# One hybrid decoder layer on eight cores: weights loaded as plain f32 and cast on ScalarE, VectorE and GpSimd, and attention's division moved into the retention stage

## The reference

```python
xn = rmsnorm(x)
qa, ka, va, qr, kr, vr, gr, ga, gb = split(xn @ w_in)
# A: 16 heads of width 64, keys by stride, three patterns (window, dilation)
for w, r in ((128, 1), (512, 4), (2048, 16)):
    num += exp(s - m) @ v        # the three share one numerator
    den += sum(exp(s - m))       # and one denominator
y_att = (num / den) @ w_att
# B: 4 heads, keys 256 wide, values 512 wide, chunks of 128 positions
y = inner_decayed @ v + (q * xi) @ state;  state = state * gamma + (k * zeta).T @ v
y_ret = (rmsnorm(y) * silu(gr)) @ w_ret
x = x + (sigmoid(ga) * y_att + sigmoid(gb) * y_ret) @ w_out
x = x + moe(rmsnorm(x))          # 4 groups of 8 experts, top 2 of the top group
```

## Time and profile before

| | |
|---|---|
| median of the runs shown | 1613.28 us (1604.24 to 1700.53, 3 runs) |
| the profiled execution itself | 1600.68 us |
| its span, first to last instruction, slowest core | 1596.2 us |
| PE busy | 1371.4 us, 86% of the span |
| DVE, ACT, POOL busy | 765.3, 695.0, 763.7 us |
| DMA queue q0 (POOL) | 124.30 MB, 48.6% of the 16 DMA engines' time |
| DMA queue q1 (SP) | 140.76 MB, 28.2% |

### The profile page before, as it was taken

The page is one execution under the profiler, slowest core; times in us unless marked ns, Lnnn a source line. Parts: engine busy times, 40 slices in busy tenths (PEclk is TensorE's granted clock), DMA queues, the critical chain, the costliest instruction groups (busy, mean ns, idle before and its releaser), DMA issues.

```text
span 1596.2 us, 29866 instructions; the slowest of 8 cores (1581.8 to 1596.2 us)
## 1 busy us (share of the span) xinstructions
PE 1371.4 (86%) x10037; PEld 787.3 (49%) x10037; DVE 765.3 (48%) x1239; ACT 695.0 (44%) x1191; POOL 763.7 (48%) x874
## 2 busy tenths in 40 slices
PE   4889998888879999999999899999999746476575
PEld 2344447777654444444444344444445435355463
DVE  3687774767556656555656411111355662121122
ACT  3576667887753444434443411111233543223232
POOL 1379991332236657666756312221226645354353
PEclk9999998999999999999999899999999867788797
DMA  9747865777865678999984299785964785999985
GB/s 213 212 92 131 166 145 152 175 175 171 176 146 100 112 107 127 127 131 146 125 134 123 55 293 175 119 131 111 261 211 166 212 303 151 265 254 256 261 188 92
DMA packets 105502, 267.03 MB, mean 167 GB/s; under 512 B 43354, under 2 KB 65370, under 8 KB 98818
## 3 DMA queue, kind: packets, MB, share of 16 engines
q0 software_dynamic: 29280, 124.30, 48.6%
q1 hardware_dynamic: 76066, 140.76, 28.2%
HBM read 285.71 MB, written 116.65 MB: 252 GB/s over the span
## 4 chain that ended last, share of the span: by engine, by line
PE 69%; DMA 14%; DVE 4%; issue 4%; ACT 4%; POOL 3%; SPq 1%; POOLq 0%; DVEq 0%; ACTq 0%
PE ps L169 69%; DMA arena<-xn,idx 8%; DMA zret<-arena 5%; ACT arena L169 4%; DVE arena L169 3%; POOL arena L169 3%; DMA arena<-x 1%; DMA cfs_sb<-cfs 1%; SPq L169 1%; DVE arena L167 1%; DMA vp<-arena 0%; ACT L169 0%; DVEq L156 0%; DVE logit L169 0%; POOL wb L169 0%
## 5 line engine op out<-in xcount | busy, mean ns | idle before, releaser
L169 PE MATMUL ps<-arena 128*128 128x512 bf16 (+5 forms) x8208 | 1275.5, 313 | 75.1 <-ACT arena L169 30.2
L169 PEld LDWEIGHTS ps<-arena 128*128 128x128 bf16 (+1 forms) x8208 | 677.4, 102 | 583.4 <-issue 121.5
L169 ACT ACTIVATE arena<-ps 128x512 bf16<-128x512 f32 (+5 forms) x600 | 422.5, 719 | 445.8 <-PE ps L169 416.7
L169 POOL TENSOR_TENSOR arena<-arena 128x512 bf16<-128x512 f32 (+4 forms) x274 | 347.8, 1278 | 296.5 <-DVE arena L169 243.0
L169 DVE TENSOR_TENSOR arena<-ps,arena 128x512 f32<-128x512 f32 (+4 forms) x420 | 235.2, 572 | 337.9 <-PE ps L169 153.5
L169 PE MATMUL ps<-cbs_sb,arena 128*128 128x128 bf16 x1408 | 130.8, 232 | 111.6 <-DMA arena<-xn,idx 76.3
L169 DVE SCALAR_TENSOR_TENSOR arena<-arena,ps 128x512 f32<-128x512 f32 x176 | 115.6, 683 | 192.8 <-PE ps L169 191.3
L169 PEld LDWEIGHTS ps<-cbs_sb,arena 128*128 128x128 bf16 x1408 | 100.3, 104 | 180.8 <-issue 152.0
L169 ACT ACTIVATE arena<-arena 128x8 f32<-128x8 f32 (+5 forms) x225 | 148.6, 665 | 60.1 <-DVE arena L169 24.5
L169 DVE TENSOR_TENSOR arena<-arena 128x1024 bf16<-128x1024 bf16 (+9 forms) x176 | 131.7, 756 | 70.6 <-ACT arena L169 63.6
L169 POOL DMA_INDIRECT out<-arena,idx x48 | 76.3, 1591 | 122.8 <-ACT arena L169 68.8
(11 more groups left out here) (60 smaller groups left out, 340.6 us busy)
## 6 DMA issues: line engine op xcount, KB each, us to landing
wb<-wexp POOLq DMA_DIRECT2D x60, 768.0 KB, 16.0
arena<-wb SPq DMA_DIRECT2D x30, 1536.0 KB, 16.0
arena<-x SPq DMA_DIRECT2D x32, 512.0 KB, 7.2
arena<-vx POOLq DMA_DIRECT2D x12, 768.0 KB, 15.1
arena<-wri POOLq DMA_DIRECT2D x8, 1024.0 KB, 23.2
zret<-arena SPq DMA_DIRECT2D x16, 512.0 KB, 19.0
arena<-zret SPq DMA_DIRECT2D x4, 2048.0 KB, 17.2
out<-arena SPq DMA_DIRECT2D x16, 512.0 KB, 8.2
```

Source lines behind the costliest of these rows:

```text
L169: ins = getattr(engobj, meth)(*a, **kw)
```

## The change

Weights: a list of tasks of 128 x 1024 f32 (512 KB) each. `stage_load` issues the next task's plain DMA on SP into one of two (attention) or three (later) 4 KB buffers; `stage_cast` issues the cast into bf16, on POOL in attention, on ACT in retention, on DVE in the merge. Each of the two is called at fixed points: twice per head in attention, twice per step in retention, five times per unit in the merge. A cast comes two (attention) or three calls behind its load. Head 0 has 12 tasks, as has each other head; a merge block has 5, the output projection 8.

Division: after a head SP stores the numerators (f32, 512 KB) and one row of denominators to DRAM. In retention DVE inverts all denominators at once (step 1, 128 x 256), and 32 units of 128 x 512 follow: loads of numerators and broadcast denominators at step 4 + u (`div_load`, three DMAs), the multiply and the store four steps later (`div_mul`). `NDB` = 4 is the number of buffers.

Masks: of the four items of dilation 4 only places 3 and 5 keep the bias matmuls; 2 and 4 take DVE's mask.

Converts: 12 in the projections, none in attention, 31 in retention (every second step to 60), 17 in the merge.

```diff
+        def stage_load():
+            n = done[0]
+            if n < len(tasks) and n - done[1] < len(stg):
+                done[0] += 1
+                i = n % len(stg)
+                p.dma(stg[i], tasks[n][1], writes=[Rstg[i]], semkey=("stg", i))
+
+        def stage_cast(eng, lag):
+            n = done[1]
+            if n < done[0] and (done[0] - n >= lag or done[0] == len(tasks)):
+                done[1] += 1
+                dst, _, r_ = tasks[n]
...
+                if eng == "act":
+                    OP("act", "activation", out=dst, in_=stg[i], func=AF.Copy, reads=[Rstg[i]], writes=[r_])
+                else:
+                    OP(eng, "tensor_copy", out=dst, in_=stg[i], reads=[Rstg[i]], writes=[r_])
...
-            if 24 <= ucount[0] < 96 and ucount[0] % 9 == 0:
+            if 24 <= ucount[0] < 96 and ucount[0] % 6 == 0:
                 convert(1)
...
-        def den_act(pr, hf, func, scale):
-            OP("act", "activation", out=den[hf], in_=den[hf], func=func, scale=scale, reads=Rden[hf], writes=Rden[hf])
...
+        def head_out(pr, e):
+            h, r0, d0, i = 2 * pr + e, e * 64, 64 - e * 64, (2 * pr + e) % NXO
+            p.dma(num_d[h * 64:(h + 1) * 64, :], xo[i][r0:r0 + 64, :], reads=Rxo[i], writes=[Rnum[h]], semkey=("zatt", i))
+            p.dma(den_d[h:h + 1, :], xo[i][d0:d0 + 1, :], reads=Rxo[i], writes=[Rdend[h]], semkey=("xin", i))
...
-            load_cast(w.rearrange("p k n -> p (k n)"), wri_d[h, :, c0:c1], 1 + j // 2, Rwr[i][j], ("wr", i, j))
+            stage_add(w.rearrange("p k n -> p (k n)"), wri_d[h, :, c0:c1], Rwr[i][j])
...
-                    if n_ == 9:
-                        convert(1)
...
-            queue.append((pr, eh, n_, S_item(pr, eh, kind, j, n_ in (2, 3, 4, 5))))
+            queue.append((pr, eh, n_, S_item(pr, eh, kind, j, n_ in (3, 5))))
...
+            if n_ in (1, 6):
+                stage_cast("pool", 2)
+                stage_load()
...
+        def div_load(u):
+            pr, qt, i = u // 4, u % 4, u % NDB
...
+        def div_mul(u):
+            pr, qt, i = u // 4, u % 4, u % NDB
+            OP("dve", "tensor_tensor", out=zo[i], in0=nb[i], in1=rb[i], op=ALU.mult, reads=[Rnb[i]] + Rrb[i], writes=[Rzo[i]])
...
                 stage_A(s_)
+                stage_cast("act", 3)
+                stage_load()
...
+                stage_cast("act", 3)
+                stage_load()
+                if s_ == 1:
+                    den_rec()
+                ud = s_ - DIV0
+                if 0 <= ud - NDB < NDV:
+                    div_mul(ud - NDB)
+                if 0 <= ud < NDV:
+                    div_load(ud)
                 pending = pending[take:]
-                if s_ % 4 != 1 and s_ < 48:
+                if s_ % 2 == 0 and s_ <= 60:
                     convert(1)
...
                 piece(fc, c, n, 4 * (un % 2), 0, "pool")
+                stage_cast("dve", 3)
+                stage_load()
...
-            if 3 <= un <= 21 and un % 2:
+            if un <= 21 and (un % 4 or un == 0):
                 convert(1)
```

More of the change, by code:

```diff
@@ L336, in psb @@
             return ps[:, b, :].bitcast(BF16)
+        late_res = set()
         def OP(eng, meth, *a, reads=(), writes=(), **kw):
@@ L341, in MM @@
         def MM(out, lhsT, rhs, start, stop, reads, writes, **kw):
+            assert not late_res or all(id(r_) not in late_res for r_ in reads)
             return p.op("pe", "matmul", (out,), dict(lhsT=lhsT, rhs=rhs, start=start, stop=stop, **kw), reads, writes)
@@ L929, in pv_next @@
             if n_ == NB - 1:
-                todo.setdefault(g + 1, []).append(lambda: (osb_copy(pr, eh, 3), den_shift(pr, eh, 1)))
-                if eh == 1:
-                    for hf in range(2):
-                        for lag, f in ((1, lambda hf=hf: den_act(pr, hf, AF.Ln, 1.0)), (3, lambda hf=hf: den_act(pr, hf, AF.Exp, -1.0)),
-                                       (5, lambda hf=hf: z_out(pr, hf) if pr < 7 else deferred.append(lambda: z_out(pr, hf)))):
-                            todo.setdefault(g + lag + 4 * hf, []).append(f)
+                todo.setdefault(g + 1, []).append(lambda: (osb_copy(pr, eh, 3), head_out(pr, eh)))
         for pr in range(2):
@@ L991, in build_nc @@
         wr_alloc(1)
+        areset(92 * KB, 96 * KB)
+        stb = [alloc([128, 1024], F32, [Rstg[0]])]
+        areset(192 * KB)
+        stb += [alloc([128, 1024], F32, [Rstg[i]]) for i in (1, 2)]
+        stage_init(stb)
         areset(112 * KB)
@@ L1138, in build_nc @@
         NWM = 3
-        Rwm = [[p.res(f"wm{i}_{j}") for j in range(2)] for i in range(NWM)]
+        Rwm = [[p.res(f"wm{i}_{j}") for j in range(5)] for i in range(NWM)]
         wm = []
@@ L1205, in build_nc @@
         wm.append(alloc([128, 40, 128], BF16, Rwm[2]))
+        stage_init([alloc([128, 1024], F32, [Rstg[i]]) for i in range(3)])
         load_wm(2)
@@ L1209, in build_nc @@
         mT = [alloc([128, 8, 512], BF16, RmT[c]) for c in range(NG)]
-        Rwo = [p.res(f"wo{i}") for i in range(2)]
-        wo = [alloc([128, 8, 512], BF16, [Rwo[0]])]
+        Rwo = [[p.res(f"wo{i}_{j}") for j in range(4)] for i in range(2)]
+        wo = [alloc([128, 8, 512], BF16, Rwo[0])]
         areset(192 * KB)
-        wo.append(alloc([128, 8, 512], BF16, [Rwo[1]]))
+        wo.append(alloc([128, 8, 512], BF16, Rwo[1]))
         Rsga = [p.res(f"sga{i}") for i in range(2)]
@@ L1223, in build_nc @@
         WMH = (slice(0, 16), slice(16, 40))
+        WMC = (slice(0, 2), slice(2, 5))
         def keep_wm(fc):
```

108 lines of the change are left out of this document (65 added, 43 removed).

## The result

The changed kernel takes 1678.19 us (median of 4 runs, 1671.34 to 1692.6) against 1611.15 us: the ratio is 1.044 with a 95% interval of [1.035, 1.054], so it is **slower**. The span of the slowest core goes from 1596.2 to 1678.8 us.

What follows compares the result with a forecast made beforehand. PE bounds retention and merge; in attention PE and ACT are both near their limit. Terms -21 - 1 - 8 + 1 + 2 + 4 + 8 + 1 = -14 us, off 1604, give 1590 us, range 1562 to 1622.

Steps and rivals of the forecast that it cites:

- The division leaves attention, -21: Attention: without the division PE's waits of 15.0 us for ACT and 5.8 us for DVE go, -21 us.
- seven divisions at 3.6 us: Attention: an alternative estimate of the division's gain, 25 us, set aside for the waits seen.
- Two of four bias pairs go, -8: Attention: dropping bias matmuls saves 12.2 us of PE, of which -8 us (0 to -12) was taken.
- Projections, +1: Projections: four more converts cost POOL 2.4 us beside its normalisation work, +1 us (0 to +3).
- Retention: DMA, +4 (0 to +25): Retention, where heads load: 17.7 us of transfers in two steps of 13.5 us, a loss of +4 us.
- ACT can lag unnoticed: Retention: ACT, idle half of the time, can lag some microseconds behind late pieces without harm.
- Merge, +8 and +1: Merge: PE waits at the first cast, +8 us (0 to +20); later blocks' pieces, +1 us (0 to +10).
- A unit and a half of slack: Merge: later blocks' pieces compete with 17 converts for 10 but have this slack, so only +1 us.
- Multiplies on DVE, +2: Retention: 32 added DVE multiplies can stand ahead of something PE needs, +2 us, bounds 0 and 28.
- The rival that they lock out POOL: Retention: DVE's multiplies delay POOL, +28 in place of +2, 1616 us in all; chance 0.08.
- The rival of the late pieces: Retention: f32 pieces come late, ACT waits and holds PE; slower than before, +20, 1624 us; chance 0.1.
- the 9.1 at which ACT waits: Retention: with three pieces in flight, landing time in us from which the late piece decides the pace.

Runs made afterwards that it cites:

- bias4: The changed kernel with all four dilation-4 items of a head keeping their bias matmuls and DVE's 32 masks for them gone; ratio to the kernel before 1.045.
- best4: best3 with conversions spread evenly (9, 6, 35, 10 by stage) and the division's store a step after its multiply; 1585.43 us against 1605.16, ratio 0.986.
- best4b: best4 with conversions 12, 6, 31, 11 by stage, four fewer in retention and three more in the projections; ratio to the kernel before 0.987.
- no_div: The changed kernel without the loads and multiplies of 28 of the 32 division units in retention; ratio to the kernel before 1.018.
- best3_f32: best3 with the division's numerators and inverses in f32 again, 32 units of 128 x 512 at the same gaps; ratio to the kernel before 1.035.
- r_cast_gap: The changed kernel with r_cast's edit and the f32 division units at steps away from the heads' loads; ratio to the kernel before 1.019.
- best3: Kernel before plus bf16 division in retention away from heads' loads, two bias pairs gone, only head 0 staged, conversions as before (8, 6, 36, 10); ratio 1.012.
- r_cast: The changed kernel with heads 1 to 3 and merge blocks 0 and 1 again loaded with a conversion in the transfer; ratio to the kernel before 1.034.
- after_sp: The changed kernel with division units loaded into buffers multiplied a step earlier, and stored a step after their multiply; ratio to the kernel before 1.043.
- cv_att: The changed kernel with six conversions moved from the merge back into attention, 11 in the merge for 17; ratio to the kernel before 1.033.
- best2_ms: The changed kernel with bf16 division away from heads' loads, conversions 12 in attention, 30 in retention, ten in the merge, merge still staged; ratio to kernel before 1.018.
- best3_ls: best3 with only the division unit's store issued a step after its multiply, conversions unchanged; ratio to the kernel before 1.005.
- gap_bf16: Changed kernel, bf16 division away from heads' loads, conversions 8, 6, 36, 10, later merge and output weights converted in transfer; 1616.9 and 1617.1 us against 1605.1, unclear.

## Why the prediction was wrong

- **The division leaves attention, -21**: right, and a little small: some 27 by bias4. The 25 of "seven divisions at 3.6 us", which I had set aside, was nearer.
- **Two of four bias pairs go, -8**: mis-sized, 1 to 4. That attention as a whole came within 2 us of its forecast is luck: this term was too large by about what the one before was too small. PE was busy 11 us less (191.8 of 216.5 us, against 202.9 of 222.0 in bias4's slowest core), but hardly got on faster; the "issue" and ACT waits above fill the place. I had named ACT and the two score slots as what is late next, and charged only 4 of the 12.2 us for it.
- **Projections, +1**: 7, and 3 to 6 in the seven other runs with the same twelve outside the slower chip. It goes when the conversions are eight again (234.2 to 234.9 in the five such runs there). I counted POOL's issue time for them and left out what they take of the DMA engines; that this is the cause is likely, but not shown, as the loss does not follow the number: nine took 240.4 us in best4, twelve 237.8 in best4b.
- **Retention: DMA, +4 (0 to +25)**: the step that failed; with the multiplies' +2 it was to be 6 and was 47. Its arithmetic stood in the text, 17.7 us of transfers in 13.5. What failed is the sentence behind it, that ACT can lag unnoticed: PE waited 43.1 us for that ACT. I charged a third of the excess of one head, and priced a unit at 2.0 where its loads alone take 2.8. no_div (-38), best3_f32 (+27 for twice the division's bytes), r_cast_gap (-37) and best4 (48 less than best3, at its bytes but for one conversion) show that the transfers and the times at which they come make the loss. r_cast shows that the form of the load is at most 11 us of it, and after_sp that taking the division's stores out of SP's waits gives nothing.
- **Merge, +8 and +1**: the first, the wait at the first cast, came as described (11.3 us, 24 us in). The second is the other failed step: the stage lost 45 in all, of which six of the seven added conversions are 33 (cv_att); the staging with ten conversions cost 16 (best2_ms). Its two numbers were at hand and I never added them: 0.83 x 208 = 173 us of transfers and seven conversions more at my own 6.5 us, 45, are 218 us for a stage of 208. "A unit and a half of slack" is no answer to a stage that has too much in it. (The casts on DVE are 38, not the 48 of the text: 30 of blocks 2 to 7 and 8 of the output projection. It changes nothing, as DVE is busy 59 of 256 us.)
- **Multiplies on DVE, +2**: not to be told from the rest. The rival that they lock out POOL is right in kind and far too small. The Trainium skill, "SBUF — State Buffer" (section "Who interferes with whom"), has a DVE instruction with two SBUF inputs contend with a GpSimd instruction that reads SBUF. The trace agrees: the same small addition on POOL takes 0.57 us by itself and 1.04 us beside one of the multiplies.

```profile
522.13 0.57 POOL L169 TENSOR_TENSOR arena<-arena,mhalf 128x1 f32<-128x1 f32 x1
...
588.26 0.68 DVE L169 TENSOR_TENSOR arena<-arena 128x512 bf16<-128x512 f32 x1
588.33 1.04 POOL L169 TENSOR_TENSOR arena<-arena,mhalf 128x1 f32<-128x1 f32 x1
```

But the instructions of POOL that stand beside a multiply are together only 8 us longer than their like elsewhere in the stage, and PE waits for POOL 1.7 us in the whole stage (3.4 before).
- **The rival of the late pieces** had the sign, and the place at which PE is held in the change. As the cause of all of it, it falls: without the pieces DVE is held instead, and 36 of the 47 us stay (r_cast). The Trainium skill, "DMA: Bandwidth & Descriptors" (section "Queues, rings and completion order"), has each engine take turns between queues packet by packet, which was to speak for the pieces with their 4 KB runs. The trace agrees in the order but not in the weight that I gave it: they land in 11.1 us, retention's store of as many bytes in 1 KB runs (a store, and so not quite its like) in 12.8, and both lie beyond the 9.1 at which ACT waits.

Open: whether the staging could be kept at no cost in best4's order (it has head 0 alone staged), what in attention fills the place of the bias pairs, how much of best4's 34 us belongs to the one conversion, and what SP's waits for retention's own store cost.

## What to carry to other kernels

Before work is moved off a busy engine by way of memory, add up the transfers of the stage that it is moved to, and of each stretch in which that stage's own loads land, against the time that the matmuls leave. Full DMA engines cost next to nothing here as long as no in-order engine needed one of their results soon (the kernel before, and best4); the change put such an engine there, and then late transfers stopped PE, whichever engine it was that waited. Even spacing of transfers that nobody waits for (here the conversions: 34 us in best4, with one conversion less) was worth more than moving the waits from one engine to another (11 us in r_cast).

## What the runs showed of the hardware

With the same division, retention takes 474 us with 36 conversions in its first 48 steps (best3), 460 when the division's store comes a step later (best3_ls), and 426 when 35 conversions are also spread over 57 steps (best4). A conversion of 0.786 MB takes 5.5 us of all engines in the merge of the changed kernel, where the earlier trace rows gave 6.5. Cores that run the same program part far in one kernel (gap_bf16's retention: 437 to 482 us) and hardly in another (best4b's: 424.8 to 425.0 us); the mean share of the DMA engines does not tell why, as it is 0.80 in both the shortest and the longest of gap_bf16's. One of POOL's small additions takes nearly twice as long beside a DVE multiply (0.57 and 1.04 us above).

The merge lost twice: PE waits 34 us for DVE, and its granted clock is on average 0.92 of the 2.4 GHz level against 0.99 in the earlier trace rows, lowest where PE had waited (0.73 from 960 to 985 us). The same matmuls are busy for 220.7 us instead of 207.7.

```profile
960.00:985.00 25.00, 13.72 (x51) 5.76 (x53) 6.88 (x10) 2.97 (x5) 5.60 (x6) 0.73 0.96 230
```
